# Routing's logits, squares and parts of x formed inside the memory's output product

## What is computed

```python
def second_block(x, ...):
    x = x + parallel_mixer(...)
    x = x + memory_cross_attention(rms_norm(x, norm_mem_w), rms_norm(mem, norm_memkv_w), ..., w_mo)
    x = x + hierarchical_moe(rms_norm(x, norm_moe_w), w_group, w_router, w_exp_gate, w_exp_up, w_exp_down)

def rms_norm(x, w, eps=1e-6):
    return x * lax.rsqrt(jnp.mean(x * x, axis=-1, keepdims=True) + eps) * w

def hierarchical_moe(h, w_group, w_router, w1, w3, w2):
    t = h.reshape(512, 1024)
    g_logits = t @ w_group                                  # 4 groups
    grp = jnp.argmax(g_logits, axis=-1)
    g_gate = softmax(g_logits)[grp]
    e_logits = einsum('nd,gde->nge', t, w_router)[grp]      # 8 experts of the group
    top_vals, top_idx = lax.top_k(e_logits, 2)
    gates = g_gate * softmax(top_vals)
    ...                                                     # tokens sorted by expert
    y = (silu(xb @ w1[e]) * (xb @ w3[e])) @ w2[e]           # 32 experts, 1024 to 512 to 1024
    y = segment_sum(y * gate, token)
```

## Time and profile before

| | |
|---|---|
| median of 3 runs | 1953.31 us (1950.06 to 1954.76) |
| the profiled execution | 1959.11 us, its span 1957.3 us |
| busy over the span | PE 1870.6 us, DVE 806.1, ACT 657.2, POOL 543.8 |
| mean granted TensorE clock | 0.98 |
| start of the last addition to `x` (L3017) | 1422.51 us |
| start of the first expert product (L3980) | 1463.01 us |
| start of the last pair's first product | 1916.89 us |

### The profile page before, as it was taken

How to read it: one execution, slowest core, us unless ns; L and a number is a source line. 1 busy time by engine, 2 the same in 40 slices (tenths; PEclk the granted TensorE clock), 3 DMA queues, 4 the chain that set the end, 5 groups by cost and what they waited for, 6 DMA issues and landing times. The chain is left out here.

```text
span 1957.3 us, 28972 instructions
## 1 busy us (share of the span) xinstructions
PE 1870.6 (96%) x11709; PEld 1380.9 (71%) x11709; DVE 806.1 (41%) x1645; ACT 657.2 (34%) x1376; POOL 543.8 (28%) x416
## 2 busy tenths in 40 slices
PE   7999999999999999998999989999979999999997
PEld 5789988888898666676878867986964444444443
DVE  4467565344322555434323254414142434233333
ACT  4553333332223555444352265534141111111110
POOL 2342143435543443273344231443220000000000
PEclk9999999999999999999999999999979999999999
DMA  5230112213132210152223221223518999999994
GB/s 163 65 88 28 44 53 91 83 44 108 54 105 80 65 50 28 44 200 97 93 78 126 64 82 37 95 87 141 204 45 350 418 414 417 418 419 419 418 419 173
DMA packets 132682, 313.40 MB, mean 160 GB/s; under 512 B 15280, under 2 KB 102080, under 8 KB 107968
## 3 DMA queue, kind: packets, MB, share of 16 engines
q1 hardware_dynamic: 132544, 311.49, 42.8%
HBM read 309.37 MB, written 2.10 MB: 159 GB/s over the span
## 5 line engine op out<-in xcount | busy, mean ns | idle before, releaser
L321 POOL TENSOR_TENSOR unit_low<-unit_ring,unit_high 128x512 fp32r<-128x512 f32 x332 | 437.2, 1342 | 766.5 <-ACT unit_high L314 766.5
L358 PE MATMUL dense<-hT,unit_high 128*128 128x512 f32 x560 | 230.0, 411 | 3.0 <-DVE dense_temps L531 1.7
L360 PE MATMUL dense<-hT,unit_low 128*128 128x512 f32 x560 | 220.7, 394 | 0.0
L359 PE MATMUL dense<-hT,unit_high 128*128 128x512 f32 x560 | 220.6, 394 | 0.0
L314 ACT CAST unit_high<-unit_ring 128x512 fp32r<-128x512 f32 x332 | 186.1, 619 | 52.5 <-PE dense L453 24.9
L451 PE MATMUL dense<-unit_high,hT 128*128 128x256 f32 x608 | 175.8, 289 | 0.7 <-POOL unit_low L321 0.4
L452 PE MATMUL dense<-unit_low,hT 128*128 128x256 f32 x608 | 172.2, 283 | 0.0
L453 PE MATMUL dense<-unit_high,hT 128*128 128x256 f32 x608 | 172.2, 283 | 0.0
L358 PEld LDWEIGHTS dense<-hT,unit_high 128*128 128x128 f32 x560 | 106.6, 190 | 29.7 <-issue 3.9
L359 PEld LDWEIGHTS dense<-hT,unit_high 128*128 128x128 f32 x560 | 106.8, 191 | 23.8 <-issue 3.1
L360 PEld LDWEIGHTS dense<-hT,unit_low 128*128 128x128 f32 x560 | 106.4, 190 | 23.0
(11 more groups left out here) (599 smaller groups left out, 3646.9 us busy)
## 6 DMA issues: line engine op xcount, KB each, us to landing
expert_ring<-w_exp_gate SPq DMA_DIRECT2D x64, 1024.0 KB, 9.9
expert_ring<-w_exp_up SPq DMA_DIRECT2D x64, 1024.0 KB, 10.5
expert_ring<-w_exp_down SPq DMA_DIRECT2D x64, 1024.0 KB, 9.3
unit_ring<-w_in SPq DMA_DIRECT2D x55, 1024.0 KB, 5.2
unit_ring<-w_mkv SPq DMA_DIRECT2D x8, 1024.0 KB, 5.5
unit_ring<-w_br SPq DMA_DIRECT2D x14, 512.0 KB, 6.3
x<-x SPq DMA_DIRECT2D x8, 512.0 KB, 5.8
w_out_raw<-w_out SPq DMA_DIRECT2D x4, 1024.0 KB, 8.9
```

What stands on the lines that cost most here:

```text
L321: nc.gpsimd.tensor_tensor(low[:, at:at + 512], raw[:, at:at + 512], high[:, at:at + 512], ALU.subtract).then_inc(*self.split.up())
L358: nc.tensor.matmul(out, high[:, k, c], rh, start=(k == 0), stop=False)
L359: nc.tensor.matmul(out, high[:, k, c], rl, start=False, stop=False)
L360: last = nc.tensor.matmul(out, low[:, k, c], rh, start=False, stop=(k == kd - 1))
```

## The change

`dense_residual` for the memory is replaced by `memory_output`, which writes routing's first work between the fills of the output product, unit by unit: when a quarter of the channels of `x` is final, TensorE transposes it (`turn`), ScalarE and VectorE copy one bank each (`keep`), and TensorE adds its share of the logits. For units 0 to 2 this share is a 36-row sum over all 512 tokens (`sum_logits`, two f32 products of 512 columns); it is copied out once, brought into the logits' bank by four small products, and the last unit's share is added by eight products as before. `split` makes the two parts of `x`, now not normalised, and the sums of squares. So the head of `moe` (`turn_x`, `route_logits`, `keep_turned`, `round_xn`, `rest_of_xn` and GpSimd's two functions) is gone.

The norm is applied later: `rs` is computed with Ln and Exp beside the choice (with Sqrt and a reciprocal before), scales the differences of logits ahead of the softmax (`scale_logits`), multiplies the gates, and reaches Silu as a per-slot scale (`slot_norm`), which `pick_pair` forms with one more reduction. For that a fifth spread (`norm_of`) is added in the first pair, the first spread moves ahead of the gathers, the others are regrouped, and ScalarE's `take_silu` waits for `pick_pair`. `pick_pair` of pair p+1 moves from the head of that pair to behind `gate_hidden` of pair p. `expand` waits per half for the gather jobs that it reads. The two parts of `x` take two places of the expert ring, two slots move to where the normalised parts were, and five items instead of six are loaded ahead of `moe`.

```diff
-        for n, token in enumerate((values_done, S.mem_scored, S.mem_scored, S.mem_jobs_turned, S.mem_mixed[3], S.mem_mixed[3])):
+        for n, token in enumerate((values_done, values_done, S.mem_scored, S.mem_scored, S.mem_jobs_turned)):
             sp.wait_ge(*token)
             experts.load(sp, n)
-    run(dense_residual(core, ring, S, "mem_o", x, [S.chunk["turned", k] for k in range(KD)]))
+    memory_output(core, ring, S, x, [S.chunk["turned", k] for k in range(KD)], route, route_landed, experts.x_parts)
+    experts.logits = S.banks[0]
...
+    def turn(i, f):
+        banks = [c[1 + 2 * (i % 2) + k] for k in range(2)]
+        @section.tensor
+        def _(pe):
+            pe.wait_ge(*added[i, f])
+            if f == 0:
+                S.take(pe, 1 + 2 * (i % 2), 2 + 2 * (i % 2))
+            for k in range(2):
+                for t in (2 * f, 2 * f + 1):
+                    last = nc.tensor.transpose(banks[k][:, t * P:(t + 1) * P], x[:, t, (2 * i + k) * P:(2 * i + k + 1) * P], core.ident)
+            last.then_inc(*turned.up())
+        return turned.now()
...
+    def keep(i, token):
+        @section.scalar
+        def _(act):
+            if i >= 2:
+                act.wait_ge(*summed_of[i - 2])
+            act.wait_ge(*token)
+            nc.scalar.copy(xT[i % 2][:, 0, :], c[1 + 2 * (i % 2)][:]).then_inc(*kept.up())
+        first = kept.now()
+        @section.vector
+        def _(dve):
+            if i >= 2:
+                dve.wait_ge(*summed_of[i - 2])
+            dve.wait_ge(*token)
+            nc.vector.tensor_copy(xT[i % 2][:, 1, :], c[2 + 2 * (i % 2)][:]).then_inc(*kept_v.up())
+        kept_of[i] = first, kept_v.now()
+        S.bank_free[1 + 2 * (i % 2)], S.bank_free[2 + 2 * (i % 2)] = kept_of[i]
+    kept_v = core.sig("route_x_kept_by_vector")
...
+    def sum_logits(i):
+        @section.tensor
+        def _(pe):
+            if i == 0:
+                pe.wait_ge(*gained.now())
+                S.take(pe, 5)
+            for k in range(2):
+                pe.wait_ge(*kept_of[i][k])
+                last = nc.tensor.matmul(sums_bank[0:36, :], w[:, 2 * i + k, :], xT[i % 2][:, k, :], start=(i == k == 0), stop=(i == 2 and k == 1))
+            last.then_inc(*summed.up())
+        summed_of[i] = summed.now()
...
+    def split(i, f):
+        tiles, cols = slice(2 * f, 2 * f + 2), slice(i * 256, (i + 1) * 256)
+        high, low = (part[:, tiles, :].rearrange("p t (k m) -> p t k m", k=KD)[:, :, :, 32 * i:32 * i + 32] for part in x_parts)
+        columns = x[:, tiles, cols].rearrange("p t (m k) -> p t k m", k=KD)
+        @section.scalar
+        def _(act):
+            act.wait_ge(*added[i, f])
+            for t in range(2):
+                last = nc.scalar.copy(high[:, t], columns[:, t])
+            last.then_inc(*parts.up())
+            if i:
+                act.wait_ge(*squares_of[f])
+            for t in (2 * f, 2 * f + 1):
+                nc.scalar.activation(junk[:, t, :], x[:, t, cols], ACT.Square, accum_out=route["sums"][:, 4 * t + i:4 * t + i + 1]
+                                     ).then_inc(*squared.up())
+        token, squares_of[f] = parts.now(), squared.now()
+        @section.vector
+        def _(dve):
+            dve.wait_ge(*token)
+            for t in range(2):
+                last = nc.vector.tensor_tensor(low[:, t], columns[:, t], high[:, t], ALU.subtract)
+            last.then_inc(*rest.up())
...
+    for i in range(4):
+        n = ring.at[f"mem_o{i}"]
+        for f in range(2):
+            got = ring.tokens(n, (2 * f, 2 * f + 1), S.hT, chunks=chunks if i == f == 0 else None)
+            ring.round(2)
+            dst = x[:, 2 * f:2 * f + 2, i * 256:(i + 1) * 256]
+            added[i, f] = ring.by_vector(got, lambda dve, bank: nc.vector.tensor_tensor(
+                dst, dst, bank[:].rearrange("p (t n) -> p t n", t=2), ALU.add))
+            if f == 1:
+                ring.finish(n)
+            if f == 0 and i:
+                keep(i - 1, turn(i - 1, 1))
+            if f == 1:
+                if i:
+                    sum_logits(i - 1)
+                turn(i, 0)
+            if (i, f) != (3, 1):
+                split(i, f)
+    @section.scalar
+    def _(act):
+        act.wait_ge(*summed_of[2])
+        nc.scalar.copy(partial[0:36, :], sums_bank[0:36, :]).then_inc(*kept.up())
+    partial_kept = kept.now()
+    token = turn(3, 1)
+    @section.tensor
+    def _(pe):
+        pe.wait_ge(*partial_kept)
+        S.take(pe, 0)
+        nc.tensor.matmul(logits[:, 0:36 * NT], partial[0:36, 0:P], first[0:36, :], start=True, stop=False)
+        for t in range(1, NT):
+            nc.tensor.matmul(logits[:, 36 * t:36 * t + 36], partial[0:36, t * P:(t + 1) * P], core.ident[0:36, 0:36], start=False, stop=False)
+    keep(3, token)
+    split(3, 1)
+    @section.tensor
+    def _(pe):
+        for k in range(2):
+            pe.wait_ge(*kept_of[3][k])
+            for t in range(NT):
+                last = nc.tensor.matmul(logits[:, 36 * t:36 * t + 36], xT[1][:, k, t * P:(t + 1) * P], w[:, 6 + k, :], start=False, stop=(k == 1 and t == NT - 1))
+        last.then_inc(*logits_s.up())
...
-    order = [("gather", 0, i) for i in range(4)]
+    order = [("spread", 0, 0)] + [("gather", 0, i) for i in range(4)]
     for p in range(N_EXPERTS // 2):
         g, q = p // 2, p % 2
         if p == 0:
-            order += [("spread", 0, i) for i in range(4)]
+            order += [("spread", 0, i) for i in range(1, 5)]
...
-    ORDER = (3, 1, 4, 6, 2, 5, 0)
+    ORDER = (0, 3, 1, 4, 6, 7, 8)
...
+        if i < 2:
+            wait_read(pe, ("gather", g, 2 * i + 1))
         if i == 0:
-            wait_read(pe, ("gather", g, 3))
...
-        nc.scalar.activation(silu[:], gate_bank[:], ACT.Silu).then_inc(*silu_s.up())
+        act.wait_ge(*pair_pick.at(p + 1))
+        nc.scalar.activation(silu[:], gate_bank[:], ACT.Silu, scale=slot_norm[:, p:p + 1]).then_inc(*silu_s.up())
...
+    def scale_logits(dve):
+        dve.wait_ge(*inverted.at(1))
+        nc.vector.tensor_tensor(diff[:], diff[:], rs[:], ALU.mult)
+        nc.vector.tensor_tensor(gexp[:], gexp[:], bc(rs[:], N_GROUPS), ALU.mult).then_inc(*chosen_s.up())
...
-        return nc.vector.tensor_tensor_reduce(flat(at_slot), flat(at_slot), flat(gate_of), 1.0, 0.0, ALU.mult, ALU.add,
-                                              slot_gate[:, p:p + 1])
+        link(nc.vector.tensor_tensor_reduce(flat(at_slot), flat(at_slot), flat(gate_of), 1.0, 0.0, ALU.mult, ALU.add,
+                                            slot_gate[:, p:p + 1]))
+        return nc.vector.tensor_tensor_reduce(at_slot[:, 0, :], out, norm_of[:], 1.0, 0.0, ALU.mult, ALU.add, slot_norm[:, p:p + 1])
...
-            turn_x(pe)
             rank_tokens(pe)
+            spread(pe, 0)
...
-                        spread(pe, i)
+                        for s in ((1,), (2, 3), (4,), ())[i]:
+                            spread(pe, s)
...
+            act.wait_ge(*totalled.at(1))
+            nc.scalar.activation(rs[:], rs[:], ACT.Ln, scale=1.0 / D, bias=core.eps[:, 0:1]).then_inc(*rooted.up())
+            act.wait_ge(*rooted.at(1))
+            nc.scalar.activation(rs[:], rs[:], ACT.Exp, scale=-0.5).then_inc(*inverted.up())
+            keep_spread(act, 0)
...
+                if p + 1 < PAIRS:
+                    pick_pair(dve, link, p + 1, float(PAIR * (p + 1)), pickT[:, (p + 1) % 2, :]).then_inc(*pair_pick.up())
```

203 lines of the change are left out of this document (68 added, 135 removed).

## The result

The changed kernel took 1943.2 us (median of five runs, 1941.74 to 1944.51); the kernel before, in the same five rounds, 1953.31 (1950.06 to 1954.76). The ratio is 0.9947, with a 95% interval of 0.9934 to 0.9961: between 7.6 and 12.9 us faster. The forecast was 1941.9 in a range of 1937.5 to 1948.5. The profiled execution of the changed kernel took 1943.2 us too, its span 1941.3.

A forecast was written before the change was run, and what follows sets the result against it. The prediction took TensorE to bound the expert stage, DMA close behind, with routing's exposed head ahead of it. Seven terms summed to −11.4 us, from 1953.3 to 1941.9, range 1937.5 to 1948.5.

The forecast's parts named there:

- Term 1: Output product: routing's transposes and sums put between its fills lengthen it by 6.7 us, without TensorE waiting.
- Rival 1: Output product: TensorE waits for its helpers' copies, cutting the gain to 6.0 us, 1947.3; chance 0.15.
- Term 2: Head of routing: last addition to `x` until the choice shrinks from 20.3 to 6.1 us, −14.2.
- Term 3: Choice to first gather: −0.4 us; `best_group` freed from GpSimd gives −0.7, the spread sticks out by 0.3.
- Term 5: First expert product: −1.1 us, since it no longer waits for the last copy of turned tokens.
- Term 4: The 64 gather products: −0.9 us, the clock coming back sooner because the spread makes TensorE busy sooner.
- Term 6: First expert pair: −1.5 us, taken between −0.9 and −2.4 by whether the clock falls after a 1.4 us wait.
- Term 7: Pairs 1 to 15: 0 us, VectorE having room for the moved pick and one more reduction.
- Rival 2: Expert stage: DMA takes over and takes back what the first pair wins, 1943.4; chance 0.07.
- Rival 3: Gathers and first pair: the clock stays at 2.4 GHz throughout, gain 14.4 us, 1938.9; chance 0.06.

The follow-up runs named there:

- e7: The changed kernel with all units' transposes, bank copies and sums of logits put behind the output product's last fill; 1942.6 us, ratio 0.9946.
- e9: The kernel before with two unread 512-column products filling TensorE's 1.8 us wait in the head of routing; 1952.3 us, ratio 0.9993.
- e6: The changed kernel with one unread subtraction added on GpSimd at the start of the choice; 1943.9 us, ratio 0.9947.
- e2: The changed kernel with the first expert product again waiting for all four copies of gathered tokens; 1943.0 us, ratio 0.9943.
- e1: The changed kernel with a one-element Silu behind the last spread's copy, loading Silu's table early; 1942.1 us, ratio 0.9944.
- e3: The changed kernel with the first spread of the slots put back behind the gathers; 1944.2 us, ratio 0.9946.
- e11: The changed kernel with two unread 1024-element copies added on VectorE ahead of the first pair's gate; 1944.8 us, ratio 0.9954.
- e8: The changed kernel with the pick of pairs 1 to 15 formed twice on VectorE; 1943.8 us, ratio 0.9952.
- run 64: Not a label but a count: the kernel before, unchanged, was run 64 times over all comparisons, with a mean of 1953.7.
- e4: The kernel before run once more, unchanged, for a second trace; 1954.4 us, ratio 1.0003.
- e5: The changed kernel with unread TensorE products added before the ranking and between ranking and spread; 1941.8 us, ratio 0.9937.

## Why the prediction was right, and where it wasn't

**Term 1** (+6.7): +6.55, with no wait on TensorE. The additions stand 6.2 and 8.2 us apart where 6.3 and 8.0 were said. So the sum came out closer than its parts: a group of transposes cost 0.43 us where I took 0.54, a pair of sums 2.0 where I took 1.7, and the two misses cancel. Rival 1 is out.

**Term 2** (−14.2): −14.2, and the start of the choice at A + 6.1 to the tenth. What the text gave as its reason was only partly right. It named the 32 logit calls "mostly at half clock" among what goes away, but placed the gain in the move. e7 shows the move itself as 0.2 us: terms 1 and 2 are −7.7 together with the work in the product and −7.5 with it behind. e9 shows that with the one wait of 1.8 us filled the head is 6.2 us shorter in the kernel before as it stands. So of the 7.5 about 6.2 are the clock, kept up through the head, and by difference about 1.3 the smaller work; the number was right, but the sum of the new head took the full clock for granted, and what the old head lost to the clock stands in it without a price.

**Term 3** (−0.4): −0.73. `best_group` gave its 0.74, and the spread that should have stuck out by 0.3 ended as VectorE's picks did. e6 confirms the cause. The term was an understatement in another sense: without the removal of GpSimd's work, a head of 14 us meets it for 4.5 us (e9: C to G 13.51 against 9.00), six times the 0.74 that the trace of before showed.

**Terms 4 and 5** (−0.9 and −1.1): −1.89 together. Term 5 is confirmed by e2 (1.0). Term 4 was 0.9 in this execution; e1, with the same code, shows 0.66 less, so that its size is 0.2 to 0.9 by executions. Its reason failed: I let the clock come back sooner because the spread makes TensorE busy sooner, but it came back at the same time after C with the spread ahead of the gathers (e1) and behind them (e3). What brought it back after 7 to 14 gather products instead of 16 no run shows, and that the number fit is luck.

**Term 6** (−1.5): −2.54. This is the term that was mis-sized. Its bounds were −0.9 and −2.4, by whether the clock falls after 1.4 us of waiting, and I took a value between them; it doesn't fall (2.57 us for transposes and second gather), and e11 shows that it falls after 2.8. The parts are −1.04 up to the transposes, −1.31 for transposes and second gather, and −0.19 in the down projection, which the sum left out (7.11 us from start to start, now 6.92). A term with two outcomes has no middle: I should have carried both with a chance. The table's 1.28 us was right (e1). The ends "of all terms together" have the same term wrong: the terms' own bounds add up to −5.7 and −15.6, and −4.9 comes out only with term 6 at −0.1, which needs the longer load that e1 rules out here.

**Term 7** (0): −0.43, some 0.03 us a pair (30.00 against 30.04 in the middle one). No run explains it. e8 shows that VectorE's queue had room for twice the pick. Rival 2 is out with the row of the middle pair: 417 GB/s, and TensorE waits for no weights. Rival 3 held for the first pair and not for the gathers: ranking and spread ran at 0.50, and seven gather products with them.

**The sum.** By the landmarks the change is worth −12.8 − 0.4 = −13.2 us where −11.4 was forecast. The medians say −10.1, with an interval of −7.6 to −12.9, so the two disagree by about 3 us, and the forecast lies between them. That the median came so near the forecast is therefore in part luck. The kernel before was run 64 times over all comparisons, with a mean of 1953.7 (76 times with e4's, the same mean); that doesn't close it. One candidate is that the kernel before has executions in which its long head is shorter, which its two traces (both 20.3 us, both with the early fall) didn't catch; half of all traces have no early fall. Another is that what lies ahead of F costs the changed kernel something, its loads of expert weights being issued at other times. As an estimate, the executions' times less the stretches from F on of their own kernel's trace (and the 1.8 or 1.9 us outside the span) put F at 1376.8 in the mean over 76 executions of before and at 1378.6 over 61 of the changed kernel and its variants; the three and eleven values of F in the traces, with means of 1378.4 and 1378.5, don't show that difference. None of this was tested. It stays open.

## What to carry to other kernels

Before moving work out of an exposed stretch, look at the granted clock in it: filling a wait of 1.8 us with products that nobody reads was worth 6.2 us of head (of which GpSimd's work let 2.3 through), and moving the changed kernel's work into the product 0.2. A cost that a slow neighbour hides, such as GpSimd's subtractions under the old head, comes out in full as soon as the neighbour is fast; price it from its own duration, not from what it costs today. Compare two traces from a landmark just ahead of the change: here most stretches of the same code repeated to 0.05 us between executions, while the way to the landmark scattered by 7. And ask first whether the two executions are of one kind: where the clock fell once just ahead of the landmark, its next fall and return came 1.5 us sooner, and a comparison across the two kinds gave e3 0.6 us that weren't its own.

## What the runs showed of the hardware

- VectorE's operation of two SBUF inputs waited for the end of GpSimd's running operation: 1.75, 2.10 and 2.77 us for 16 elements per partition, ends within 0.05 us of each other. I had expected contention, not a wait to the very end.
- TensorE's clock fell after waits of 1.05 and 1.80 us close together, after 2.38 (three traces) and after 2.81 (one), not after one of 1.36 (seven traces). The length of the wait alone didn't decide: after the same 1.64 us ahead of F it was low in seven of 14 traces, and in e5 it fell while TensorE worked, behind a wait of 0.36 us.
- At the choice it fell 0.6 us after C and came back 10.8 us after it in four traces, and fell about 2 us and came back 12.0 to 12.3 us after C in four others, with the spread in either place and with the gathers 1.6 us late. With products added there that nobody reads it came back 4.0 us after C (e5).
- A load of Silu's table cost 1.28 us, and an early Silu of one element took all of it off the path.
- The first addition to `x`, 1380 us into the span, lay at 1374.96 to 1382.19 in 14 traces, with offsets that arose in steps; one of them, about 1.6 us, was the clock's fall just ahead of it.
